# Later starts for eight of the sixteen groups of weight sums in a one-core encoder step (Trainium2)

## The chip, the cores and the metric
The kernel runs on one core of one Trainium2 chip. The metric is the device time of one execution in microseconds (us), from three runs. Five engines work side by side, each on its own list of instructions, and meet only at semaphores: PE (TensorE, matmuls), DVE (VectorE) and ACT (ScalarE, both elementwise work), POOL (GpSimd) and SP (SyncE, which here only issues loads). Transfers of all of them run on the same 16 DMA engines.

## The reference, cut to what matters
```python
# one layer, 544 tokens (512 prompt + 32 sample), D_MODEL 1024, all float32
xn = rms_norm(x, g_mix);  h = xn @ w_in                  # u, q, k, v, gates
y_pool = multiscale_pool(...); o = stick_breaking(q,k,v) # 8 heads x 64
x = x + (gate_a * (y_pool @ w_pool_up) + gate_b * (o @ w_sb_up)) @ w_out
x = x + square(relu(rms_norm(x, g_mlp) @ w_up)) @ w_down # w_up 1024x4096, w_down 4096x1024
x = x + sigmoid(rms_norm(x, g_ple) @ w_ple_gate) * (p @ w_ple_proj)
y = rms_norm(x, g_final)
```

## The kernel before, in words
The weights come in tiles of 128 partitions x 1024 float32 (512 KB). SP loads each into a raw buffer, ACT copies it into `w_hi` (a rounded part, L845 or L853), DVE subtracts to get `w_lo` (L1812 or L1820), and PE multiplies with both parts (three passes for one float32 product). `w_hi` and `w_lo` are rings of four tiles (`W_RING`), so ACT may fill the place of tile t once PE has finished tile t-4.

The order of the work is: the input projection with the eight heads of attention (to about 255 us), the pooled and the attended halves of the mix (to about 307), the output projection `out` of eight tiles of 6 us (307 to 355), four chunks of the MLP, the embedding gate (`ple`), the end. In a chunk c come two "up" groups (2c and 2c+1) and, in chunks 0 to 2, two interleaved "down" groups. Each group is a 2x2 block product done with **seven** products instead of eight (Winograd's form), in the order of the sides A11, S1, S2, S4, S3, A12, A22. One product takes PE 3 us. Down groups run in pairs: side 0 of e=0, side 0 of e=1, side 1 of e=0, and so on, fourteen products. The last chunk's down projection is a plain one.

The sides S1 to S4 are sums of the four quarters of the weights. They are made by POOL's DMAs, from DRAM to DRAM, into `sums_t`: four plain copies of quarters (step 0, L782), then four DMAs that add to what stands there (steps 1 to 3, two, one and one, L789). There are sixteen such groups, in this order of `SUM_GROUPS`: up0, up1, dn0, dn1, up2, up3, dn2, dn3, up4, up5, dn4, dn5, up6, up7, ple0, ple1 (index 0 to 15). POOL goes through numbered **slots** k. In slot k it waits until the DMAs of all earlier slots have landed, issues the copies of the group that begins there, then the additions that are due of groups begun before. Slots 0 to 7 stand behind the masks of the eight heads. From slot 8 on each has a pace, a number of results that PE must have finished (`full`), one for the copies and one for the additions:

- slot 8: none; 9: the attended half's start and its middle; 10: the output projection's start and its middle
- slots 11, 13, 15, 17: the first and the second up group of chunk 0, 1, 2, 3
- slots 12, 14, 16: side 0 and side 4 of the down pair of chunk 0, 1, 2; slot 18: the same of chunk 3

In the kernel before, group i begins in slot i, so that it is complete with slot i+3.

SP loads the tiles of the later stages in their order of use (`staged`), into six raw buffers. For a side S1 to S4 it first waits until every DMA of every slot up to the last one of that group has landed (the wait at L679), and everything behind it in SP's order waits too. A raw buffer is free once DVE has made `w_lo` of the tile six places earlier.

In a down pair DVE's and ACT's order is, for product j (of 14): make the split of tile j+3 (`ahead(j)`), then take the result of product j out of PSUM (`second_taken`, L2262):
```python
for j in range(2 * T_UP):
    ...
    ahead(t_dn(c, j // 2, j % 2))
    ...
    second_taken(c, j // 2, j % 2)
```
PE starts a product only when the weights are split (`weights`) and the PSUM place it writes has been taken (`place_for`). There are four places; side A22 of e=0, the thirteenth product (j = 12) of a down pair, uses place 0, and so does side A11 of the following even up group.

Of the kernel before, what the change touches and what calls it, by code (L numbers as in the profile page):

```python
# [19 lines left out]
HEADS = 8  # L20
# [66 lines left out]
SUM_STEPS = ((("S1", "A21"), ("S3", "A21"), ("S2", "A11"), ("S4", "A12")), (("S1", "A22"), ("S3", "A11")),  # L87
             (("S2", "S1"),), (("S4", "S2"),))

SUM_GROUPS = tuple((what, 2 * c + e) for c in range(CHUNKS) for what in ("up", "dn") if what == "up" or c < SEVENS  # L90
                   for e in range(2)) + (("ple", 0), ("ple", 1))

SUM_PAD = 16

# [63 lines left out]
def t_dn(c, s, e):  # L158
    return T_MLP + c * T_CHUNK + 2 * T_UP + 2 * s + e


def t_down(c, q):
    return T_MLP + c * T_CHUNK + 2 * T_UP + q


def t_ple(g, s):
    return T_PLE + g * (T_UP + 1) + PLE_PLACE[g][s]


def t_group(g, s):  # L170
    return t_up(g, s) if g < UP_GROUPS else t_ple(g - UP_GROUPS, s)
# [31 lines left out]
def group_side(name):  # L203

    if name[0] == "dn":
        return ("dn", 2 * name[1] + name[3]), SIDES[name[2]]
    if name[0] in ("down", "proj", "p"):
        return None
    g, what = name
    return ("up", g) if g < UP_GROUPS else ("ple", g - UP_GROUPS), what  # L210


def stored_tile(name):

    if name[0] == "down":
        return T_MLP + 16 * name[1] + 8 + name[2]
    if name[0] == "proj":
        return T_MLP + 16 * CHUNKS + 5 * name[1] + 4
    (stage, g), what = group_side(name)
    return quarter_tile(stage, g, what)  # L220
# [77 lines left out]
def hybrid_step_kernel(nc, w_tiles, x_t, p_t, ck_t, cv, state_t, w_grp, vecs,  # L298
# [5 lines left out]
    with ctx:  # L304
# [3 lines left out]
        def sem(name):  # L308
            return ctx.enter_context(nc.semaphore(name))
# [156 lines left out]
        def raw_at(n):  # L466

            return (n + RAW_RING) % RAW_BUFS

        def raw_buf(n):  # L470
            b = raw_at(n)
            return raw[:, b, :] if b < RAW_RING else raw_more[:, b - RAW_RING, :]
# [23 lines left out]
        def tokens(i):  # L496
            return slice(i * HALF, (i + 1) * HALF)
# [24 lines left out]
        sums_in = sem("sums_in")  # L522
# [98 lines left out]

        def sum_slot(k):

            return [(i, k - i) for i in range(max(0, k - len(SUM_STEPS) + 1), min(k + 1, len(SUM_GROUPS)))]

        def sums_made(k):

            return 16 * sum(len(SUM_STEPS[step]) for j in range(k + 1) for _, step in sum_slot(j))
# [7 lines left out]
        @block.sync  # L636
        def _(sp):

            first = (("w", 0), ("x", 0), ("w", 2), ("x", 1), ("x", 2), ("x", 3), ("w", 1), ("x", 4), ("w", 3),
                     ("x", 5), ("x", 6), ("x", 7))  # L640
            for what, n in first:
                if what == "x":
                    sp.dma_start(xt[:, n, :], x_t[n, :, :]).then_inc(x_in[n], 16)
                else:
                    t, part = n // 2, slice(n % 2 * D_MODEL // 2, (n % 2 + 1) * D_MODEL // 2)
                    sp.dma_start(raw[:, t, part], w_tiles[t, :, part]).then_inc(half_in[n] if n < 3 else raw_in[1], 16)

            with sp.Fori(1, T_OUT // RAW_RING + 1) as r:
                for s in range(RAW_RING):
                    sp.wait_ge(wlo_done, r * RAW_RING + (s - RAW_RING + 1))  # L650
                    sp.dma_start(raw[:, s, :], w_tiles[r * RAW_RING + s, :, :]).then_inc(raw_in[s], 16)

            def wait_free(n):

                if n < RAW_BUFS - RAW_RING:
                    sp.wait_ge(yblo_done, 2)
                elif n < RAW_BUFS:
                    sp.wait_ge(wlo_done, T_MLP - RAW_RING + raw_at(n) + 1)
                else:
                    name = STAGED_LOADS[n - RAW_BUFS]  # L660
                    if name[0] == "dn":
                        sp.wait_ge(wlo_done, t_dn(*name[1:]) + 1)
                    elif name[0] == "down":
                        sp.wait_ge(wlo_done, t_down(name[1], name[2]) + 1)
                    elif name[0] == "p":
                        sp.wait_ge(ptlo_done, name[1] + 1)
                    elif name[0] == "proj":
                        sp.wait_ge(wlo_done, t_ple(name[1], T_UP) + 1)
                    else:
                        g, what = name  # L670
                        sp.wait_ge(wlo_done, t_group(g, SIDES.index(what)) + 1)

            def staged(n):
                name = STAGED_LOADS[n]
                wait_free(n)
                group, what = group_side(name) or (None, None)
                if what in SUMS:
                    nth = SUM_GROUPS.index(group)
                    sp.wait_ge(sums_in, sums_made(nth + len(SUM_STEPS) - 1))  # L679
                    sp.dma_start(raw_buf(n), sums_t[len(SUMS) * nth + SUMS.index(what), :, :])\  # L680
                        .then_inc(raw_in[raw_at(n)], 16)
                elif name[0] == "p":
                    sp.dma_start(raw_buf(n)[:, 0:TOK], p_t[:, name[1], :]).then_inc(raw_in[raw_at(n)], 16)
                else:
                    sp.dma_start(raw_buf(n), w_tiles[stored_tile(name), :, :]).then_inc(raw_in[raw_at(n)], 16)


            for j, t in enumerate(range(T_OUT + RAW_RING, T_MLP)):
                sp.wait_ge(wlo_done, t - RAW_RING + 1)
                sp.dma_start(raw[:, t % RAW_RING, :], w_tiles[t, :, :]).then_inc(raw_in[t % RAW_RING], 16)  # L690
                for n in range(2 * j, min(2 * j + 2, RAW_BUFS - RAW_RING)):
                    staged(n)
            for n in range(RAW_BUFS - RAW_RING, len(STAGED_LOADS)):
                staged(n)
            for nth, i in enumerate((1, 0)):

                for m in (4, 2, 0, 6) if nth else (0, 4, 2, 6):
                    if m == 0:
                        sp.wait_ge(fin_pool, 2 * nth + 2)
                    else:  # L700
                        sp.wait_ge(fin_done, len(BY_DVE) * nth + BY_DVE.index(m) + 1)
                    for two in range(2):
                        sp.dma_start(y_t[m + two, :, tokens(i)], xt[:, m + two, tokens(i)]).then_inc(out_done, 16)
            sp.wait_ge(out_done, 16 * 2 * KT)

        @block.gpsimd
        def _(pool):
# [67 lines left out]
            def sum_copies(k):  # L775

                if 0 < k:
                    pool.wait_ge(sums_in, sums_made(k - 1))
                for i, step in sum_slot(k):
                    if step == 0:  # L780
                        for what, of in SUM_STEPS[0]:
                            pool.dma_start(sum_tile(i, what), sum_tile(i, of)).then_inc(sums_in, 16)  # L782

            def sum_additions(k):

                for i, step in sum_slot(k):
                    if step:
                        for what, of in SUM_STEPS[step]:
                            pool.dma_start(sum_tile(i, what), sum_tile(i, of), accum_op=ALU.add).then_inc(sums_in, 16)  # L789
# [21 lines left out]
            paces = [(0, 0), (N_ATT, N_ATT + KT // 2), (N_OUT, N_OUT + KT // 2)]  # L811
            for c in range(CHUNKS):
                second = [NTH[("dn", c, s, 0)] for s in (0, 4)] if c < SEVENS else [NTH[("down", c, q)] for q in (0, 4)]
                paces += [(NTH[("up", 2 * c, 0)], NTH[("up", 2 * c + 1, 0)]), tuple(second)]
            for k, (copies, additions) in enumerate(paces, HEADS):
                if copies:
                    pool.wait_ge(full, copies)
                sum_copies(k)
                if copies:
                    pool.wait_ge(full, additions)  # L820
                sum_additions(k)
# [1732 lines left out]
```

## Time and profile before
| | us |
|---|---|
| median of 3 runs | 774.92 (773.32 to 775.55) |
| the profiled execution, its own time | 772.34 |
| its span, first to last instruction | 770.6 |
| PE busy | 754.8 (98%) |
| DVE, ACT, POOL busy | 556.9, 422.0, 147.2 |
| granted TensorE clock, mean | 0.996 |

Everything below is read from that one profiled execution; times of day are us from the start of its span. Busy time of PE counts overlapping matmuls once. A DMA's "landing" is the time from its issue until its semaphore has been raised.

### The profile page before, as it was taken

How to read it: one execution, taken by the hardware profiler on the slowest of the kernel's cores; microseconds unless marked ns; L12 is line 12 of the kernel's file. 1: busy time of each engine (PE TensorE's matmuls, PEld its weight loads, DVE VectorE, ACT ScalarE, POOL GpSimd, SP SyncE). 2: the span in 40 equal slices, each digit the busy share in tenths (PEclk: the TensorE clock that was granted, in tenths of full speed). 3: DMA queues.
4: the chain of work that ended last, by engine and by line, in shares of the span. 5: the costliest groups of instructions: out<-in, count | busy, mean ns of one | idle time of the engine just before them, and what ended most of it. 6: DMA issues, size and time to landing. Idle time of an engine off the chain costs nothing.

```text
span 770.6 us, 14459 instructions
## 1 busy us (share of the span) xinstructions
PE 754.8 (98%) x5902; PEld 746.2 (97%) x5902; DVE 556.9 (72%) x705; ACT 422.0 (55%) x524; POOL 147.2 (19%) x259
## 2 busy tenths in 40 slices
PE   9999999999999999999999999999999999999994
PEld 9999999999999999999999999999999999999993
DVE  6776556566567527588998669965998667677986
ACT  7545535435485442477674347634763356556575
POOL 1051342453471332021110111111101000000001
PEclk9999999999999999999999999999999999999998
DMA  7254848769779899988797989789776957342503
GB/s 242 93 181 140 233 147 224 225 193 262 218 179 265 259 242 275 292 267 262 213 299 270 236 329 251 282 232 354 207 243 201 278 185 217 105 117 66 204 1 116
DMA packets 49516, 165.78 MB, mean 215 GB/s; under 512 B 6320, under 2 KB 8368, under 8 KB 49456
## 3 DMA queue, kind: packets, MB, share of 16 engines
q1 hardware_dynamic: 28512, 94.16, 35.6%
q0 software_dynamic: 18688, 67.18, 35.5%
q10 hardware_dynamic: 2256, 3.60, 1.4%
q8 instruction: 43, 0.70, 0.4%
q14 instruction: 17, 0.14, 0.1%
HBM read 160.39 MB, written 71.63 MB: 301 GB/s over the span
## 4 chain that ended last, share of the span: by engine, by line
PE 90%; DVE 5%; ACT 3%; issue 1%; DMA 1%; SPq 0%; POOL 0%; POOLq 0%; DVEq 0%
PE psum L1646 23%; PE psum L1697 16%; PE psum L1345 14%; PE psum L1351 14%; PE psum L1348 14%; PE psum L1394 1%; PE psum L1422 1%; DMA xt<-x_t 1%; PE psum L1420 1%; PE psum L1382 1%; PE psum L1381 1%; ACT xt L1265 1%; PE psum L1401 1%; PE psum L1406 1%; ACT L879 0%
## 5 line engine op out<-in xcount | busy, mean ns | idle before, releaser
L853 ACT ACTIVATE w_hi<-raw_more 128x1024 fp32r<-128x1024 f32 x83 | 87.7, 1056 | 72.3 <-PE psum L1697 43.3
L1345 PE MATMUL psum<-a_hi,w_hi 128*128 128x272 f32 x576 | 120.6, 291 | 0.6 <-DVE w_lo L1812 0.5
L1820 DVE TENSOR_TENSOR w_lo<-raw_more,w_hi 128x1024 fp32r<-128x1024 f32 x83 | 101.1, 1222 | 26.1 <-ACT w_hi L853 25.7
L1351 PE MATMUL psum<-a_hi,w_lo 128*128 128x272 f32 x576 | 119.3, 289 | 0.0
L1348 PE MATMUL psum<-a_lo,w_hi 128*128 128x272 f32 x576 | 118.9, 288 | 0.0
L1646 PE MATMUL psum<-u_hi,w_hi 128*128 128x272 f32 x560 | 116.4, 289 | 1.0 <-ACT h_of L1097 1.0
L1646 PE MATMUL psum<-u_hi,w_lo 128*128 128x272 f32 x560 | 115.8, 289 | 0.0
L1646 PE MATMUL psum<-u_lo,w_hi 128*128 128x272 f32 x560 | 115.7, 288 | 0.0
L1345 PEld LDWEIGHTS psum<-a_hi,w_hi 128*128 128x128 f32 x576 | 90.3, 189 | 1.1 <-DVE w_lo L1812 0.7
L1348 PEld LDWEIGHTS psum<-a_lo,w_hi 128*128 128x128 f32 x576 | 90.5, 189 | 0.0
L1351 PEld LDWEIGHTS psum<-a_hi,w_lo 128*128 128x128 f32 x576 | 90.0, 189 | 0.0
L1646 PEld LDWEIGHTS psum<-u_hi,w_hi 128*128 128x128 f32 x560 | 87.9, 188 | 1.7 <-issue 1.2
L1646 PEld LDWEIGHTS psum<-u_lo,w_hi 128*128 128x128 f32 x560 | 88.3, 189 | 0.0
L1646 PEld LDWEIGHTS psum<-u_hi,w_lo 128*128 128x128 f32 x560 | 87.4, 188 | 0.0
L1812 DVE TENSOR_TENSOR w_lo<-raw,w_hi 128x1024 fp32r<-128x1024 f32 x41 | 51.2, 1250 | 43.3 <-ACT w_hi L845 43.1
L1820 DVE TENSOR_TENSOR w_lo<-raw,w_hi 128x1024 fp32r<-128x1024 f32 x44 | 53.6, 1222 | 19.2 <-ACT w_hi L853 12.3
L789 POOL DMA_DIRECT2D sums_t<-sums_t x32 | 27.5, 1013 | 207.1 <-PE psum L1646 87.9
L1348 PE MATMUL psum<-b_lo,w_hi 128*128 128x272 f32 x304 | 62.9, 288 | 0.0
L853 ACT ACTIVATE w_hi<-raw 128x1024 fp32r<-128x1024 f32 x39 | 41.2, 1056 | 36.0 <-PE psum L1697 21.6
L1345 PE MATMUL psum<-b_hi,w_hi 128*128 128x272 f32 x288 | 60.0, 290 | 0.0
L782 POOL DMA_DIRECT2D sums_t<-w_tiles x64 | 33.6, 535 | 135.5 <-DMA sums_t<-w_tiles 97.7
L1351 PE MATMUL psum<-b_hi,w_lo 128*128 128x272 f32 x288 | 59.4, 287 | 0.0
(287 smaller groups left out, 1553.0 us busy)
## 6 DMA issues: line engine op xcount, KB each, us to landing
sums_t<-w_tiles POOLq DMA_DIRECT2D x96, 512.0 KB, 8.2
raw<-w_tiles SPq DMA_DIRECT2D x63, 512.0 KB, 4.4
raw_more<-sums_t SPq DMA_DIRECT2D x42, 512.0 KB, 5.8
raw_more<-w_tiles SPq DMA_DIRECT2D x41, 512.0 KB, 4.5
sums_t<-sums_t POOLq DMA_DIRECT2D x32, 512.0 KB, 11.1
raw<-sums_t SPq DMA_DIRECT2D x22, 512.0 KB, 6.0
xt<-x_t SPq DMA_DIRECT2D x8, 272.0 KB, 5.7
y_t<-xt SPq DMA_DIRECT2D x16, 136.0 KB, 1.9
```

The lines of the kernel that those rows point to most:

```text
L782: pool.dma_start(sum_tile(i, what), sum_tile(i, of)).then_inc(sums_in, 16)
L789: pool.dma_start(sum_tile(i, what), sum_tile(i, of), accum_op=ALU.add).then_inc(sums_in, 16)
L853: act.activation(w_hi[:, t % W_RING, :, :].rearrange("p k c -> p (k c)"), src, ACT.Copy)\
L1265: act.activation(x, x, ACT.Copy, scale=g_fin[:, m:m + 1]).then_inc(xg_last, 1)
L1345: pe.matmul(base[:, h, :], w_hi[:, s, wk, :], at(hi, k, h * HALF, (h + 1) * HALF), start=(opens and q == 0), stop=False, skip_group_check= ...
L1348: pe.matmul(base[:, h, :], w_hi[:, s, wk, :], at(lo, k, h * HALF, (h + 1) * HALF), start=False, stop=False, skip_group_check=True)
L1351: mm = pe.matmul(base[:, h, :], w_lo[:, s, wk, :], at(hi, k, h * HALF, (h + 1) * HALF), start=False, stop=(closes and q == len(ks) - 1), s ...
L1381: pe.matmul(z, b_lo[:, keys], b_hi[:, both], start=(b != 3), stop=False, skip_group_check=True)
L1646: mm = pe.matmul(out[:, two, :], w_part[:, t % W_RING, 2 * k + two, :], u_part[:, op, k, :], start=(OPENS[s] and k == 0 and w_part is w_hi ...
L1697: mm = pe.matmul(out[:, two, :], w_part[:, t % W_RING, 2 * k + two, :], h_part[:, i * HALF:(i + 1) * HALF], start=(OPENS[s] and k == 0 and ...
L1812: dve.tensor_tensor(w_lo[:, s, :, :].rearrange("p k c -> p (k c)"), raw[:, t % RAW_RING, :], w_hi[:, s, :, :].rearrange("p k c -> p (k c)" ...
L1820: dve.tensor_tensor(w_lo[:, t % W_RING, :, :].rearrange("p k c -> p (k c)"), src, w_hi[:, t % W_RING, :, :].rearrange("p k c -> p (k c)"), ...
```

## The change
A table `BEGINS` says in which slot each group begins. The first eight groups begin in slots 0 to 7 as before. The others (indices 8 to 15: up4, up5, dn4, dn5, up6, up7, ple0, ple1) begin in slots 10, 11, 11, 12, 13, 13, 14, 15 instead of 8, 9, 10, 11, 12, 13, 14, 15. The slots' paces are the same, and so are the DMAs and their number; SP's wait for a group goes to the group's new last slot.
```diff
+BEGINS = tuple(range(8)) + (10, 11, 11, 12, 13, 13, 14, 15)
+SLOTS = BEGINS[-1] + len(SUM_STEPS)
...
         def sum_slot(k):
-            return [(i, k - i) for i in range(max(0, k - len(SUM_STEPS) + 1), min(k + 1, len(SUM_GROUPS)))]
+            return [(i, k - at) for i, at in enumerate(BEGINS) if 0 <= k - at < len(SUM_STEPS)]
...
                     nth = SUM_GROUPS.index(group)
-                    sp.wait_ge(sums_in, sums_made(nth + len(SUM_STEPS) - 1))
+                    sp.wait_ge(sums_in, sums_made(BEGINS[nth] + len(SUM_STEPS) - 1))
...
-            for k, (copies, additions) in enumerate(paces, HEADS):
+            for k, (copies, additions) in zip(range(HEADS, SLOTS), paces):
```

## Rows read from the trace of the kernel before
**Rows 1.** The page, part 1: busy us, share, instructions.
```profile
PE 754.8 (98%) x5902; PEld 746.2 (97%) x5902; DVE 556.9 (72%) x705; ACT 422.0 (55%) x524; POOL 147.2 (19%) x259
```
**Rows 2.** PE's waits, the longest: who waited for whom, us, times, longest.
```profile
PE psum L1781 <- ACT h_two L1310: 1.9, 1, 1.9
```
**Rows 3.** Windows: stretch, then busy us by engine, PEclk, DMA share, GB/s.
```profile
307.00:355.00 48.00, 48.00 (x385) 48.00 (x385) 37.16 (x54) 28.02 (x37) 7.27 (x11) 1.00 0.98 282
```
**Rows 4.** SP's waits: the one for sums of weights.
```profile
SPq L679 <- DMA sums_t<-w_tiles: 4.2, 1, 4.2
```
**Rows 5.** Timeline of POOL, additions of slots 14, 15, 16: start, length, instruction.
```profile
508.93 1.70 POOL L789 DMA_DIRECT2D sums_t<-sums_t  x2 [21.60 <-PE psum L1697]
...
547.98 1.70 POOL L789 DMA_DIRECT2D sums_t<-sums_t  x2 [17.11 <-PE psum L1646]
549.07 1.45 POOL L789 DMA_DIRECT2D sums_t<-w_tiles  x1
560.95 0.81 POOL L789 DMA_DIRECT2D sums_t<-w_tiles  x1 [10.44 <-issue]
593.65 1.64 POOL L789 DMA_DIRECT2D sums_t<-sums_t  x2 [31.90 <-PE psum L1697]
594.71 2.25 POOL L789 DMA_DIRECT2D sums_t<-w_tiles  x2
```
**Rows 6.** Timeline of SP: loads of up5, dn4 and dn5, up6, up7.
```profile
526.09 3.35 SPq L680 DMA_DIRECT2D raw<-sums_t  x2
...
553.77 7.03 SPq L680 DMA_DIRECT2D raw_more<-sums_t  x4
...
589.55 6.33 SPq L680 DMA_DIRECT2D raw_more<-sums_t  x3
...
612.14 1.79 SPq L680 DMA_DIRECT2D raw_more<-sums_t  x2
```
**Rows 7.** DMA queues, 552 to 556: packets, MB, share (q0 POOL's, q1 SP's).
```profile
q0 software_dynamic: 222, 0.84, 106.9%
```
**Rows 8.** The same view, 509 to 529.
```profile
q0 software_dynamic: 576, 2.10, 57.0%
q1 hardware_dynamic: 838, 3.08, 42.1%
```
**Rows 9.** The same view, 595 to 611.
```profile
q0 software_dynamic: 572, 2.09, 70.5%
q1 hardware_dynamic: 522, 1.89, 30.9%
```
**Rows 10.** SP's loads into raw_more: one at 612.1, then those of 570 to 580.
```profile
DMA to landing us min/median/max: 4.4/4.4/4.4
...
DMA to landing us min/median/max: 3.4/3.4/3.5
```
**Rows 11.** Timeline of ACT, splits of up5's S1, dn5's S1, up6's S1.
```profile
541.77 1.06 ACT L853 ACTIVATE w_hi<-raw 128x1024 fp32r<-128x1024 f32 x1 [1.94 <-PE psum L1646]
...
572.13 1.04 ACT L853 ACTIVATE w_hi<-raw_more 128x1024 fp32r<-128x1024 f32 x1
...
605.21 1.06 ACT L853 ACTIVATE w_hi<-raw_more 128x1024 fp32r<-128x1024 f32 x1 [1.94 <-PE psum L1697]
```
**Rows 12.** Timeline of DVE: up6's S1 split, then the thirteenth down result taken.
```profile
606.31 1.23 DVE L1820 TENSOR_TENSOR w_lo<-raw_more,w_hi 128x1024 fp32r<-128x1024 f32 x1 [0.36 <-ACT w_hi L853]
608.18 0.72 DVE L2262 TENSOR_TENSOR xt<-xt,psum 128x544 f32<-128x544 f32 x1 [0.64 <-PE psum L1697]
```
**Rows 13.** Timeline of PE: first matmuls of up6, then its last of all.
```profile
611.00 0.42 PE L1646 MATMUL psum<-u_hi,w_hi 128*128 128x272 f32 x2
...
760.40 1.19 PE L1781 MATMUL psum<-h_two,negone 128*128 128x272 f32 x4 [1.85 <-ACT h_two L1310]
```
**Rows 14.** Windows at the end of the span, as rows 3.
```profile
760.00:764.00 4.00, 1.19 (x4) 0.68 (x4) 3.40 (x7) 2.50 (x7) 0.00 (x0) 1.00 0.76 258
764.00:768.00 4.00, 0.00 (x0) 0.00 (x0) 1.99 (x3) 0.40 (x1) 1.48 (x2) 0.57 0.52 180
```

## The prediction
> **What bounds the kernel now.** I read the page's busy times first. PE is busy 754.8 of 770.6 us [rows 1]: it is the bound, and only its 15.8 us of idle time can be won. Next came PE's waits. The longest is 1.9 us and lies in the last stage [rows 2]; the seven in the list sum to 6.7 us and none is for a DMA. So no transfer holds PE up today. Third came busy time by stretch, for the place that the change empties. In the output projection PE is busy 48.00 of 48.00 us although the DMA engines are 98% busy [rows 3]; the stretch 276 to 307 shows the same. The crowding there costs PE nothing. Fourth, the queue that feeds PE: SP waited for sums of weights once, 4.2 us, before up7's S1 [rows 4], whose load went out at 612.14 [rows 6]. That wait is the warning. The kernel has slack between sums and their loads, and at one place it is already gone. So the question is which loads lose how much slack.
>
> **The change, part by part.** The same 64 copies and 64 additions are issued. POOL's instruction time is unchanged, and POOL does nothing between the sample's masks and its last products but these DMAs.
>
> *What is taken away.* Slot 8 loses 4 copies; slots 9 and 10 together keep 3 additions and 4 copies of their 16 DMAs. Gain: between nothing, since PE does not idle there [rows 3], and the 1.9 us of PE's longest wait anywhere [rows 2]. I take nothing, the row of the place itself.
>
> *What is added later.* Counting steps with the new table: slot 12 has 5 additions (4 before), slot 13 has 8 copies and 5 additions (4 and 4), slot 14 has 7 additions (4), slot 15 has 5 (4), slot 16 has 5 (4), slot 17 two and slot 18 one, as before. Slot 11 has 8 copies and 2 additions.
>
> *What an addition costs.* With POOL's queue alone on the DMA engines it moves 222 packets in 4 us [rows 7], 55.5 a us. Four additions are 576 packets [rows 8], 144 each, so one takes 2.6 us. First packets come some 3 us after the first issue (32 packets stand between 595 and 597, after 593.65). In 509 to 529, 20 us held 4 additions and 838 / 144 = 5.8 loads [rows 8]; less 3 us of start and 10.4 of additions leaves 6.6, or 1.1 us per load that shares the engines. Check on slot 16 as it was: 593.65 + 3 + 10.4 + 3.6 loads x 1.1 [rows 9] = 611.0, where the load that waited for it went out at 612.14 [rows 6]. The rule is 1 us short, which I keep in mind.
>
> *Who waits for whom.* The new last slots: up4 slot 13 (was 11), up5 14 (12), dn4 14 (13), dn5 15 (14), up6 16 (15), up7 16 (16), ple0 and ple1 unchanged.
> - up4: complete with slot 13, by my count near 490, one chunk ahead of its load (up5's went out at 526.09 [rows 6], up4's a group earlier, at 505). No cost.
> - up5: slot 14's additions go out at 508.93 [rows 5]: + 3 + 7 x 2.6 + 6.5 loads x 1.1 = 537. Its S1 load went out at 526.09 [rows 6] and now goes at 537, beside four copies. It lands about 542 to 543; ACT wanted it at 541.77 [rows 11]. PE needs it split at 550.9 (up5 starts at 547.8, S1 is its second product), so some 5 us of cover remain. Cost 0; if slot 14 ran 8 us later, 3 us.
> - dn5: slot 15's additions at 547.98 [rows 5]: + 3 + 13 + 3 loads x 1.1 = 567.5. The load lands about 572; ACT split it at 572.13 [rows 11]. No cover is left on ACT, about 2 us on PE. I take 0.4, between 0 and 3.
> - up6: **this one breaks.** Before, its sums were complete with slot 15; the S1 load went out at 589.55 [rows 6]. Now they are complete with slot 16, whose additions are paced by PE's eighth down product and go out at 593.65 [rows 5], four us after the load used to. SP is stopped at this load from 589.55, so it issues nothing and the additions have the DMA engines alone: 593.65 + 3 + 13 + 0.3 = 610.0. The load: 0.1 + 4.4 [rows 10], landed at 614.5. ACT 1.06 [rows 11], DVE about 1.2. But DVE's order in a down pair is split first, take afterwards: the take of the thirteenth down result, at 608.18 before, stands behind this split (606.31) [rows 12], and up6's A11 writes the PSUM place that this take frees. So PE can't start up6 at 611.00 [rows 13]: it starts at 614.5 + 0.1 + 1.06 + 0.1 + 1.15 + 0.72 + 0.1 = 617.7. Stall: **6.7 us**. Behind it nothing adds up: the five next loads are in flight together, up7's sums are complete with the same slot, and A11's own 3 us cover the S2 split. A stall here isn't won back, since PE has no idle time after it to take it from.
>
> Bounds of that stall: below, additions as taken and a load of 3.4 us [rows 10], 5.7; the nearest row above is slot 16 with loads beside it, four additions in 18.5 us, 4.6 each, so five end at 616.8 and the stall is 13.5. I take 6.7, since nothing shares the engines, the condition of rows 7.
>
> *The clock.* PE's last matmul ends at 761.6 [rows 13]; the granted clock is 1.00 (2.4 GHz) in 760 to 764 and 0.57 in 764 to 768 [rows 14], so it fell to its lower level (1.2 GHz) with PE idle, less than 7 us after that matmul. A stall of 6.7 us may do the same in the middle, and then PE works at half rate for a while. No row shows a rise. Below: 0. Above: if the low level lasts as long as the tail that this span shows, 6 us, 3 us are lost. I take 1.5. The Trainium skill (TensorE: Matmul & The Clock Gate, Part 1) says that an engine left idle goes to the lower level and returns only after sustained work; by that the loss is sure to be above nothing, and its size is what this trace can't show; the fall at the end agrees.
>
> The page DMA: Bandwidth & Descriptors of the Trainium skill (section on the fixed cost of a DMA) gives 2.0 us and bytes / 436e3 for one transfer, 3.2 us for 512 KB; by that the load would land 1.2 us earlier and the stall be 5.5. The trace's 4.4 for a lone load differs, and the sum goes by it.
>
> *Sum.* 6.7 + 1.5 + 0.4 = 8.6 us on the profiled execution's 772.34, 780.9; its span 770.6 becomes 779.2. The runs' median is 2.6 above that execution, so I forecast **783.5** for the median.
>
> **The rivals.**
> 1. *More than one stall.* Slot 14's seven or slot 15's five additions end later than I count (my rule is 1 us short on slot 16), and up5 or dn5 holds PE too. For: no cover on ACT at dn5. Against: the additions speed up as soon as SP stops. It gives 3 to 5 us more, 788.
> 2. *Only the weights bind.* If the take isn't behind the split, PE runs A11 from 611.0 and waits for S1 alone: 614.5 + 2.4 = 616.9 against 614.0, 2.9 us, no fall of the clock: 777.8. For: the ring is made for this slack. Against: the order in rows 12.
> 3. *POOL stops in slot 16.* In slot 15 the last addition came 10.44 us late, "issue", with no releaser [rows 5]. It was the 121st sum DMA, and it went out just as POOL's queue had drained. A shorter such gap stands before the 77th. If it is a matter of counting, it falls on the first addition of slot 16 now; the queue is long drained there, so it should cost nothing. If the wait is 10 us regardless, up6 is late by 10 us more: 794.
> 4. *The other side: not slower.* The five additions of slot 16 would have to be done by 603.4 (for a landing at 607.8 and a take at 611). That leaves 9.8 us from 593.65; at 2.6 us each plus 3 us of start they need 16. It decides from 1.4 us an addition down. Then the emptied stretch could at best return a few tenths: 774.5. The same time would come if the groups weren't moved in effect.
>
> **How the numbers follow.** One stall as summed 0.64; rival 1 0.14; rival 2 0.09; rival 3 0.05; rival 4 0.08, of which 0.05 within 0.3% (2.3 us, about what a measurement of this kernel can tell from no change) and 0.03 faster. Rival 2's 777.8 is 0.4% slower; runs differ by a us, so a tenth of it goes to "same". The forecast's own range is 780 to 787 (5.7 without any clock cost, less a us; and 9 with 3). Reaching to rivals 1 and 2: 778 to 791, which leaves out rivals 3 and 4 and edges.
>
> **What would show it.** In the trace after: one long wait of PE at the first matmul of up6 (L1646), released by DVE's take at L2262, 5 to 9 us; SP's wait at L679 near 20 us long before up6's S1, with smaller ones of about 11 us before up5's and before dn5's; slot 16's five additions with POOL's queue alone on the engines, 16 us from first issue to that load; the granted clock below 1.00 in the stretch behind the stall; no gap in POOL's issue in slots 15 and 16; PE still fully busy from 276 to 355. Wrong I am if SP's wait is there and PE's isn't (the cover is larger than I read), or if PE's idle time stands at up5 or dn5.

## The result and the profile after

The changed kernel takes 780.88 us (median of 4 executions, 780.47 to 781.87) against 775.0 for the kernel before: a ratio of 1.0081, 95% interval 1.0063 to 1.01. In a second, separate measurement it took 781.8 us, ratio 1.0078 (1.005 to 1.0105). It is slower by 5.9 us and lies inside the forecast range (778 to 791). The traced execution took 780.65 us, 8.3 more than the traced one of before (772.34).

PE's waits in the kernel after (who waited for whom, total us, times, longest). Line numbers of this kernel are four higher than those of before. The first line is new; the second stands as it did in [rows 2].
```profile
PE psum L1650 <- DVE xt L2266: 6.2, 1, 6.2
PE psum L1785 <- ACT h_two L1314: 1.9, 1, 1.9
```
SP's waits for sums. Where there was one of 4.2 us [rows 4] there are three: 14.6 us before up5's S1, 16.3 before dn5's and 22.0 before up6's.
```profile
SPq L683 <- DMA sums_t<-w_tiles: 52.9, 3, 22.0
```
The chain that ended last, 600 to 624 us (start, length, what): from the last addition of slot 16 to PE, link by link.
```profile
597.08 13.99 DMA sums_t<-w_tiles
611.08 0.02 issue
611.09 0.02 SPq L683
611.11 0.03 issue
611.14 3.45 DMA raw_more<-sums_t
614.59 0.02 issue
614.61 1.06 ACT w_hi L857
615.67 0.02 issue
615.70 1.23 DVE w_lo L1824
616.92 0.64 DVE xt L2266
617.57 0.14 issue
617.70 6.30 PE psum L1650 x36
```
That is the path of the forecast: sums, load, split on ACT, split on DVE, the take of the thirteenth down result, and only then up6's first product, at 617.70 instead of 611.00 [rows 13].

POOL's additions in slots 14, 15 and 16 (timeline), seven, five and five, for [rows 5]:
```profile
509.28 0.84 POOL L793 DMA_DIRECT2D sums_t<-sums_t  x1 [18.52 <-PE psum L1701]
510.31 1.66 POOL L793 DMA_DIRECT2D sums_t<-sums_t  x2 [0.19 <-issue]
511.38 3.92 POOL L793 DMA_DIRECT2D sums_t<-w_tiles  x4
...
548.33 2.52 POOL L793 DMA_DIRECT2D sums_t<-sums_t  x3 [7.33 <-PE psum L1650]
549.94 2.58 POOL L793 DMA_DIRECT2D sums_t<-w_tiles  x2
594.98 2.49 POOL L793 DMA_DIRECT2D sums_t<-sums_t  x3 [42.47 <-issue]
596.56 2.60 POOL L793 DMA_DIRECT2D sums_t<-w_tiles  x2
```
SP's loads after (timeline): up5's sums, then dn4's and dn5's, then up6's, for [rows 6]. They went out at 538.45 (before 526.09), the second of the down pair with a gap inside the 17.99 us, and at 611.14 (589.55).
```profile
538.45 0.80 SPq L684 DMA_DIRECT2D raw<-sums_t  x2
...
554.12 17.99 SPq L684 DMA_DIRECT2D raw_more<-sums_t  x4
...
611.14 1.28 SPq L684 DMA_DIRECT2D raw_more<-sums_t  x3
```
The granted clock around the stall (windows, columns as rows 3). It is at its lower level (0.50, 1.2 GHz) when PE starts again and back at 1.00 after 622; at the lower level PE gets through 10 matmuls in 2 us, at the higher through 18.
```profile
612.00:616.00 4.00, 0.00 (x0) 0.00 (x0) 0.30 (x1) 1.16 (x2) 0.00 (x0) 0.79 0.97 338
616.00:618.00 2.00, 0.30 (x1) 0.33 (x2) 2.00 (x3) 1.64 (x2) 0.00 (x0) 0.50 1.03 418
618.00:620.00 2.00, 2.00 (x10) 2.00 (x10) 2.00 (x3) 0.37 (x1) 0.00 (x0) 0.50 1.02 418
620.00:622.00 2.00, 2.00 (x14) 2.00 (x13) 0.45 (x1) 0.00 (x0) 0.00 (x0) 0.72 1.03 414
622.00:624.00 2.00, 2.00 (x18) 2.00 (x18) 0.00 (x0) 1.41 (x2) 0.00 (x0) 1.00 0.98 385
```
The stretch that the change empties, for [rows 3]: the DMA engines go from 98% to 57%, and PE stays busy for all 48.00 us.
```profile
307.00:355.00 48.00, 48.00 (x386) 48.00 (x385) 37.85 (x54) 28.29 (x37) 2.90 (x5) 1.00 0.57 194
```
Where the 8.3 us of the traces are: slot 17's additions, paced by PE, go out at 641.04 instead of 632.71, 8.33 later, and the span is 8.3 longer. Of that 0.35 was there by slot 15 (548.33 against 547.98) and 6.2 are the wait. The rest, 1.8, is found by subtraction and put down to the low clock, the only other thing that the windows show between.

### The profile page after: what moved, and what is told of

It reads as the page before. It is cut to its first block, busy times and chain, and to the rows that moved or that the text cites. A ratio compares the mean times of both kernels' runs of the same rounds, so it can differ in the third digit from the quotient of the medians.

```text
span 778.9 us, 14459 instructions
## 1 busy us (share of the span) xinstructions
PE 756.6 (97%) x5902; PEld 747.7 (96%) x5902; DVE 557.2 (72%) x705; ACT 422.4 (54%) x524; POOL 146.1 (19%) x259
## 4 chain that ended last, share of the span: by engine, by line
PE 82%; issue 6%; DVE 5%; DMA 3%; ACT 3%; POOL 1%; POOLq 0%; SPq 0%; DVEq 0%
PE psum L1650 23%; PE psum L1701 14%; PE psum L1349 13%; PE psum L1355 13%; PE psum L1352 13%; DMA sums_t<-w_tiles 2%; PE psum L1398 1%; PE psum L1426 1%; PE psum L1424 1%; DVE w_lo L1824 1%; PE psum L1386 1%; PE psum L1385 1%; ACT xt L1269 1%; ACT w_hi L857 1%; ACT L883 0%
## 5 line engine op out<-in xcount | busy, mean ns | idle before, releaser
L1824 DVE TENSOR_TENSOR w_lo<-raw_more,w_hi 128x1024 fp32r<-128x1024 f32 x83 | 101.1, 1222 | 35.9 <-ACT w_hi L857 35.6
L1824 DVE TENSOR_TENSOR w_lo<-raw,w_hi 128x1024 fp32r<-128x1024 f32 x44 | 53.6, 1221 | 16.1 <-ACT w_hi L857 13.7
L857 ACT ACTIVATE w_hi<-raw 128x1024 fp32r<-128x1024 f32 x39 | 41.2, 1057 | 34.7 <-PE psum L1701 20.4
L849 ACT ACTIVATE w_hi<-raw 128x1024 fp32r<-128x1024 f32 x46 | 48.2, 1051 | 15.0 <-PE psum L1355 8.7
```

Source lines behind the costliest of these rows:

```text
L849: act.activation(w_hi[:, s, :, :].rearrange("p k c -> p (k c)"), raw[:, t % RAW_RING, :], ACT.Copy).then_inc(whi_done, 1)
L857: act.activation(w_hi[:, t % W_RING, :, :].rearrange("p k c -> p (k c)"), src, ACT.Copy)\
L1824: dve.tensor_tensor(w_lo[:, t % W_RING, :, :].rearrange("p k c -> p (k c)"), src, w_hi[:, t % W_RING, :, :].rearrange("p k c -> p (k c)"), ...
```

## The experiments

**Put up6 back (two measurements).**
```diff
-BEGINS = tuple(range(8)) + (10, 11, 11, 12, 13, 13, 14, 15)
+BEGINS = tuple(range(8)) + (10, 11, 11, 12, 12, 13, 14, 15)
```


> One number of the changed kernel's table is put back: up6 begins in slot 12 again, not 13, and so is complete with slot 15; the other seven groups stay where the change put them. Theory (the stall at up6 is the whole cost): SP's wait before up6's S1 goes, PE's long wait at up6 goes, the granted clock stays at 1.00, and the median is that of the kernel before, 775 us, at most 0.5 above it. Rival (the crowding of DMAs from slot 11 on costs something at up5, dn5 and in other places too): 777 to 779 us. Rival (the emptied stretch of slots 8 to 10 gives something that the stall hid): below 774 us.

Measured: 772.89 us (10 executions, 772.1 to 774.11), ratio 0.9984 (0.9968 to 1.0). There is no long wait of PE; its waits are those of the kernel before, and the span is 770.7. So one number of the table holds the loss. The median is 1.3 us under the 774.19 of the kernel before, which is the second rival's side (below 774), with an interval that just reaches 1. SP's waits for sums are still there:
```profile
SPq L683 <- DMA sums_t<-w_tiles: 33.6, 3, 16.5
```
They cost PE nothing in this trace, so up5's and dn5's late loads are hidden. Repeated with more executions:

> The changed kernel with up6 put back to slot 12, unchanged from its first run, with more executions. Theory (the emptied stretch removes the late loads that cost the kernel before 4.4 us at the start of the MLP in about half of its executions, and nothing else is late): no execution above 774.5 us, median 772.5 to 773.5 us, 0.997 to 0.998 of the kernel before. Rival (dn5's sums, which now have no cover, take back part of it): median 774 us, some executions with 1 to 2 us more.

Measured: 774.07 us (11 executions, 772.81 to 775.02), ratio 0.9992 (0.9982 to 1.0002). This is nearer to the rival: the median is its 774, two executions are above 774.5, and the interval holds 1. The traced execution shows what the rival names, though small: PE waits 0.5 us in the down pair for a split (L1701 for L1824), at the place where dn5's load has no cover.

**Move up6 alone.**
```diff
+BEGINS = tuple(range(12)) + (13, 13, 14, 15)
```


> The kernel before with one group moved: up6 begins in slot 13, all others as before. Slots 8 to 12 are as crowded as before, slots 14 and 15 have four additions. Theory (up6 is the whole cost): slot 16 has the same five additions as the changed kernel's, they go out at about 593.7 us and SP's load follows some 16 us later; PE waits 6 to 6.5 us at up6 and the median is that of the changed kernel, 781 us within 1. Rival (half of the cost is the general crowding): 777 to 778 us.

Measured: 783.08 us (4 executions, 781.69 to 784.27), ratio 1.0111 (1.0079 to 1.0143). The wait alone makes the whole loss, as the theory has it; the time is 2 us over the 781 that it gave. The two intervals (1.0079 to 1.0143 here, 1.0063 to 1.01 for the changed kernel) overlap, so that this kernel is slower than the changed one is likely, not shown. The row is PE's long wait:
```profile
PE psum L1650 <- DVE xt L2266: 6.7, 1, 6.7
```

**Take first, split second.**
```diff
                 for j in range(2 * T_UP):
+                    if j == 12:
+                        second_taken(c, j // 2, j % 2)
                     ahead(t_dn(c, j // 2, j % 2))
...
-                    second_taken(c, j // 2, j % 2)
+                    if j != 12:
+                        second_taken(c, j // 2, j % 2)
```


> The changed kernel with one order turned round on DVE: in the down pairs the thirteenth result (j = 12) is taken out of PSUM before the split of the tile three further on, not after it. Theory (PE stands because the take that frees its PSUM place is behind the late split): PE starts up6's first product on time at about 611.4 us and then waits only for the second product's weights, 2.5 us from 614.4 to about 616.9; the clock doesn't fall in so short a wait, so the median is 2.5 to 3 us over the kernel before, about 778. Rival (PE waits for the weights in either order): 781 us as the changed kernel, with the clock down to 0.5 again.

Measured: 777.69 us (10 executions, 776.19 to 779.41), ratio 1.0038 (1.0023 to 1.0054). PE starts up6 on time, at 610.96 (611.00 before), and stops at the second product instead. The wait shrank from 6.2 to 3.3 us and has another releaser: the weights, not the take. So DVE's order is shown to make 2.9 us of the wait, a little under half of it; the other 3.3 are the late weights.
```profile
PE psum L1650 <- DVE w_lo L1824: 3.3, 1, 3.3
```
The clock, which I had expected to hold, fell in these 3.3 us (windows of this kernel, same columns), and PE is slow until past 622. From slot 15's to slot 17's additions this trace takes 91.1 us, against 84.7 before: 3.3 for the wait and, by subtraction, 3.1 for the clock. It is the slowest of the ten executions; their mean clock runs from 0.989 to 0.995, so it did not cost all of them as much.
```profile
616.00:618.00 2.00, 0.56 (x2) 0.57 (x3) 1.79 (x2) 1.47 (x3) 0.00 (x0) 0.70 1.02 420
618.00:620.00 2.00, 2.00 (x11) 2.00 (x10) 2.00 (x3) 2.00 (x3) 0.00 (x0) 0.50 1.03 420
```

**Issue slot 16's additions earlier.**
```diff
+                if c == 2:
+                    second = [NTH[("dn", c, 0, 0)], NTH[("dn", c, 0, 0)]]
                 paces += [(NTH[("up", 2 * c, 0)], NTH[("up", 2 * c + 1, 0)]), tuple(second)]
```


> The changed kernel with the pace of slot 16's additions moved from the eighth product of the third down pair to that pair's start, so that they go out as soon as slot 15's DMAs have landed, at about 571 us in place of 595. Theory (the stall is only the distance between these additions and the load that needs them): they land by about 590, SP's load of up6's S1 goes out at 590, no wait of PE, median 775 to 775.5 us. Rival (additions beside the down pair's loads make those late instead): a wait of PE between 577 and 611 us, 777 us or more.

Measured: 774.21 us (10 executions, 773.6 to 775.5), ratio 1.0 (0.9982 to 1.0017). The additions went out at 572.26, up6's load at 598.50, where 590 was expected (other loads of SP stood before it, and the sums came 2.3 us after those), and the long wait is gone. The rival has a small share: three waits of 0.5 us in the down pair (this kernel's lines are two higher again).
```profile
PE psum L1703 <- DVE w_lo L1826: 1.6, 3, 0.5
```

**One addition fewer in slot 16.**
```diff
+BEGINS = tuple(range(12)) + (13, 13, 14, 14)
```


> As the kernel in which only up6 is moved to slot 13, and besides ple1 begins in slot 14, one earlier, so that slot 16 has four additions in place of five (slot 15 then has six). Theory (PE's wait is the additions of slot 16 by 2.6 us each): SP's load of up6's S1 goes out 2.6 us earlier relative to the first of these additions, 13.8 us behind it in place of 16.4, and PE's wait falls from 6.7 to about 4 us; the clock falls again, since it did in a wait of 3.3 us, so the median is 779 to 780.5 us. Rival (the wait is the distance from the pace to the load whatever stands between): PE's wait stays at 6 to 7 us, 783.

Measured: 778.62 us (10 executions, 776.46 to 781.15), ratio 1.005 (1.003 to 1.007). First addition at 594.00, load at 607.28: 13.3 us, against 16.4 us (595.54 to 611.93) where up6 alone was moved. So one addition is worth 3.1 us here, where 2.6 was expected. PE waits 2.7 us and not 4: the first addition also went out 1.5 us sooner, and PE came to its wait only 0.6 us sooner. That the number of additions sets the wait is shown; the median is just under the range given (779 to 780.5). The low clock is there again: 0.51 in 616 to 618.
```profile
PE psum L1650 <- DVE xt L2266: 2.7, 1, 2.7
```

**Both mends together** (up6 back, take first).

> The changed kernel with up6 put back to slot 12 and with the thirteenth down result taken before the split. It has the emptied slots 8 to 10 and no late group. Theory (the emptied stretch gives a us on average, by taking away what holds PE up at the start of the MLP in some executions): 772.9 us and no execution above 774.5, 0.998 of the kernel before, the interval below 1. Rival (the 1.3 us seen with up6 put back were chance): within 0.5 us of the kernel before.

Measured: 774.07 us (12 executions, 771.51 to 774.81), ratio 0.9988 (0.9973 to 1.0003). Neither holds: two executions are above 774.5 and the interval holds 1, but the median is 0.9 us under the 774.95 of the kernel before. PE has two waits in the down pair behind dn5's late split, 0.7 us together.

**POOL's gap.** In slot 15 of the kernel before the 121st sum DMA went out 10.44 us late [rows 5]. With up6 put back it is again the last of slot 15 and 14.24 us late. In the one with an addition fewer the 121st is the last but one, and both stand behind a gap of 13.57 us:
```profile
565.43 1.65 POOL L793 DMA_DIRECT2D sums_t<-w_tiles  x2 [13.57 <-issue]
```
In the changed kernel it is the first of slot 16, and there it went out at 594.98, where the pace alone (593.65 plus the 0.35 of shift) gives 594.0. The kernel that moves up6 alone repeats this: the 121st is the first of slot 16 there too and goes out 46.65 us after slot 15's first addition, as in the changed kernel, against 45.67 before. So it is a matter of counting, and costs 1 us when the queue is empty.

**Why the medians differ by 5.9 us and the traces by 8.3.** The executions of the kernel before spread over 771.9 to 777.5 us: of 76 timed beside the experiments 27 are under 774 and 27 at 775.5 or over. Three more traces of it were taken, to have one of each sort.

> The kernel before, unchanged, for a second trace of it: its 25 timed executions lie between 771.9 and 776.9 us and the one on the page was one of the quick ones. Theory (crowding before the MLP costs time in some executions): if this one is over 774 us, PE has waits between 300 and 390 us that the first trace lacks, behind loads that land late. Rival (the spread is at the start, in the loads of x, or at the end): PE's extra waits lie before 60 us or after 700.

> The kernel before, unchanged. Its 54 timed executions so far fall in two heaps, about 772.5 and about 776 us, and both traces of it are of the first heap. Looked for: a trace of the second. Theory (the crowded stretch makes a load late in some executions): if this one is over 775 us, PE has a wait of 2 to 4 us between 300 and 390 us that the other traces lack. Rival (it is elsewhere): the wait stands in another stretch, or spread out over matmuls with no wait.

> As the third trace of the kernel before: a further chance at an execution over 775 us, with the same two readings.

Measured: 772.52, 772.65 and 777.13 us. The third, e10, has what was looked for (PE's waits, then the windows):
```profile
PE psum L1646 <- issue: 2.8, 2, 2.2
```
```profile
354.00:358.00 4.00, 1.76 (x14) 1.57 (x13) 3.96 (x7) 3.33 (x5) 1.77 (x4) 1.00 0.60 178
358.00:362.00 4.00, 4.00 (x22) 4.00 (x21) 3.10 (x6) 2.32 (x4) 0.30 (x1) 0.58 0.98 349
```
PE stops for 2.2 us where the MLP starts, the clock falls, and the later paces are 4.5 to 4.8 us later than in the quick traces (slot 12's additions at 429.26, not 424.42 or 424.76). The loads behind it are those of the output projection's tiles: ACT waited 7.8 us for one and 3.2 for the last in this trace, where it waited 4.5 and 1.1 in the first trace of this kernel, and 0.2 once in the changed kernel. DVE splits these tiles and takes results in one order; it doesn't catch up, and PE starts up0 0.10 us behind the end of DVE's take of the seventh result of the output projection (`out`):
```profile
342.31 1.06 ACT L845 ACTIVATE w_hi<-raw 128x1024 fp32r<-128x1024 f32 x1 [3.22 <-DMA raw<-w_tiles]
356.86 0.72 DVE L2139 TENSOR_TENSOR xt<-psum,xt 128x544 f32<-128x544 f32 x1
357.68 0.54 PE L1646 MATMUL psum<-u_hi,w_hi 128*128 128x272 f32 x2 [2.24 <-issue]
```
The profile names no releaser for this wait ("issue"), but by the kernel's table of PSUM places that result lies in place 0, the one that up0's A11 writes: the mechanism of up6 once more, a take behind a late split. The other crowded traces have the lateness with no wait or one of at most 0.3 us; in the quick ones of the kernel before the same take has ended by 353.1, before PE needs the place (355). DVE's second take in the output projection stands at 327.2 to 330.5 in the four traces of the kernel before and in the two kernels that move up6 without emptying slots 8 to 10, and at 323.3 to 323.9 in all seven traces with the emptied slots. So the stretch that the change empties does make DVE late each time that it is crowded, and in some executions that reaches PE. Does more crowding cost more?
```diff
+BEGINS = tuple(range(8)) + (8, 8, 9, 9, 12, 13, 14, 15)
```


> The kernel before with more crowding in the stretch that the change empties: groups 8 and 9 both begin in slot 8, groups 10 and 11 both in slot 9, the rest as before. Slots 8 and 9 then have eight copies each. No group is later than before. Theory (crowding there costs PE something at the start of the MLP): PE waits at the output projection or at up0 (L1697 or L1646's first products, or L1345's), 1 to 5 us in all, median 776 to 779 us. Rival (the loads there have slack enough): 774 to 775 us, as before.

Measured: 774.03 us (10 executions, 773.6 to 774.93), ratio 0.9993 (0.9976 to 1.001): the rival. PE has a wait of 1.4 us more, in which the clock stays at 1.00, and no execution reaches 775. DVE's second take is on time there (323.33) and the third is late (333.32, against 328.6 to 329.1 with the emptied slots). In this kernel slot 10 has no copies, and slot 11 none either; whether it is slot 10 that decides was not tried.

The changed kernel once more:

> The changed kernel, unchanged, with more executions, since its gap in the medians was 5.9 us and its gap in the traces 8.3. Theory (the kernel before has executions that lose about 4 us, and the changed one has none of them): the changed kernel's executions lie within 2 us of each other near 781, 8.3 over the quick heap of the kernel before and some 6.5 over its median. Rival (the changed kernel varies just as much): two heaps here too, 4 us apart.

Measured: 781.8 us (4 executions, 780.11 to 785.15). The executions lie 5 us apart, so the theory (within 2 us) fails, and four don't show whether there are two heaps. The traced one took 785.15, and besides up6's wait (7.0) it has waits that the first trace lacks, in the down pair where dn5's load has no cover. Slot 16's additions are 2.2 us later by them (597.15 against 594.98):
```profile
PE psum L1701 <- DVE w_lo L1824: 1.6, 2, 1.1
```
So this kernel varies too, by another cause, and that cause is the prediction's rival 1.

## Why the prediction was right

- *up6.* Summed: additions done at 610.0, load landed at 614.5, PE at 617.7. Measured: 611.1, 614.6, 617.70. That the last of these agrees to a tenth is luck, as two small errors cancel: the additions began 1.3 us later than before (0.35 of shift, 1 of POOL's gap), and the load took 3.45 us, not 4.4 (the lone load of [rows 10] was a poor stand-in; the 3.4 of its second line was the better one). The 3.2 us that the prediction works out from the Trainium skill (DMA: Bandwidth & Descriptors) is nearer to 3.45 as well, but the page's fit is for transfers that GpSimd issues, and this load is SP's. From first addition to the end of the sums it is 16.1 us, against 16.35 in the sum. The wait is 6.2 and not 6.7, since PE came 0.4 us later. That the take stands behind the split is shown by turning it round (3.3 us left; rival 2's figure for that was 2.9).
- *The clock.* I took 1.5, a choice between 0 and 3; the trace gives 1.8. That it is so near is luck in part: PE works at 0.6 of its pace at the low clock (11 matmuls in 2 us against 18), not at half, and another trace lost 3.1. The clock falls with waits of 2.2, 2.7 and 3.3 us too, so rival 2, which says that it doesn't, was priced too low. Its 777.8 and the 777.69 measured with the take first agree by luck: it adds the 2.6 us of the median's distance, of which that kernel's trace shows nothing, and leaves out the clock, which its trace shows.
- *up5.* Load at 538.45, summed 537; no wait of PE. SP's waits before up5's and dn5's S1 were 14.6 and 16.3 us, where about 11 was forecast; PE's cover was enough for that in the first trace. *dn5.* Summed 567.5 for the load and 572 for its landing; ACT's split began at 574.30, having waited 1.73 us for it, and DVE waited 1.29. PE has no wait in the first trace, and 1.1 and 0.5 in the second, which lost 2.2 us there: the 0.4, from 0 to 3, was fair. This is rival 1, and it is real in part of the executions.
- *Rival 3.* It is a matter of counting, as read, and cost 1 us where nothing was forecast.
- *The gain of the emptied stretch, taken as 0.* This is the term that was mis-sized. It hides in the last step of the sum, which adds the 2.6 us between the traced execution and the median of before to the changed kernel as well. The traced execution of before was one of those that lose nothing at the MLP's start; another lost 4.5 us there, and none of the seven traces with the lighter slots does. Moving up6 alone costs 8.9 us by the medians (783.08 against 774.19), the changed kernel 5.9 and 6.3; the 2.6 to 3 between them are the estimate of the gain, about the distance of the forecast (783.5) from the result. That the emptying brings DVE back on time is shown by its second take in all traces; that this is worth 2.6 to 3 us of the median is not shown, since the intervals overlap and the test with more crowding did not make it worse.

Putting up6 back gives a kernel with the gain and without the loss: over both measurements its 21 executions have a median of 773.3 us and a largest of 775.02, ratios 0.9984 and 0.9992. That is one or two parts in a thousand, at the edge of what these intervals can tell, as both reach 1.

## What to carry to other kernels

When work is moved later in a queue that another engine waits on, add up, for each consumer, pace + issue + transfers of the whole group + its own load, and set that against the time at which the consumer's engine needs it. Look also at what stands behind the late instruction in each engine's order: here a take of a finished result, unrelated to the weights, added 2.9 us to a wait of 3.3. One traced execution shows one of several ways that a kernel runs; a stretch without idle time in it is no proof that the stretch never costs any.

## What was not expected of the hardware

- The granted clock fell to its lower level (0.50) with waits of PE as short as 2.2, 2.7 and 3.3 us, in the two shorter ones only as PE began again (PE at 357.68, the clock 0.99 in 357 to 358 and 0.50 in 358 to 359). By subtraction it cost 1.5 to 3.1 us on top of the wait. It did not fall in one of 1.4 us. The Trainium skill (TensorE: Matmul & The Clock Gate, Part 1) says that an idle engine goes to it, and these traces agree.
- POOL's issue of its DMAs stops at the 121st of these 512 KB transfers: 10.4 to 15.3 us with earlier ones in flight, and 1 us with none. In the kernel before it goes on as the queue has drained: POOL's queue has 33 packets in 559 to 560, 8 in 560 to 561, none in 561 to 562, and the issue came at 560.95. Gaps at other counts are short: 0.3 us before the 77th in the kernel before, with three copies just issued, and 0.2 to 0.4 before the 106th in every kernel with a changed table. What sets these counts is open.
- An addition from DRAM to DRAM of 512 KB takes the 16 DMA engines for 2.6 to 2.8 us when alone (144 packets an addition; 676 packets between 598 and 611 in the changed kernel, 52 a us, against 55.5 in [rows 7]):
```profile
q0 software_dynamic: 676, 2.44, 96.0%
```
